# The first window attention: GpSimd stores each block of outputs two steps of its loop later

## The reference, cut to what matters

```python
def _sink_probs(parts, sink):
    snk = jnp.broadcast_to(sink.astype(jnp.float32).reshape(Hk, G)[None, :, :, None, None], base.shape[:-1] + (1,))
    p = jax.nn.softmax(jnp.concatenate(list(parts) + [snk], axis=-1), axis=-1)
    return p[..., :-1]
```

## Time and profile before

| | |
|---|---|
| median of 3 runs | 2663.86 us (2663.03 to 2664.27) |
| profiled execution, its own time | 2663.9 us |
| span of its trace | 2661.8 us (2.1 us of the time lie outside) |
| busy | PE 97%, DVE 57%, ACT 30%, POOL 8% of the span |
| chain of work that ended last | PE 92%, DVE 3%, ACT 2%, issue 2% |
| the window stage | from 167.66 us (first scores) to 353.80 us (first product of the next stage) |

### The profile page before, as it was taken

How to read it: one execution, slowest core, us unless ns; L and a number is a source line. 1 busy time by engine, 2 the same in 40 slices (tenths; PEclk the granted TensorE clock), 3 DMA queues, 4 the chain that set the end, 5 groups by cost and what they waited for, 6 DMA issues and landing times.

```text
span 2661.8 us, 37526 instructions
## 1 busy us (share of the span) xinstructions
PE 2579.5 (97%) x14026; PEld 1886.8 (71%) x14026; DVE 1525.1 (57%) x3904; ACT 802.3 (30%) x1756; POOL 222.7 (8%) x401
## 2 busy tenths in 40 slices
PE   6998899999999999999999999999999999999999
PEld 3476668877768787556678777778678866555867
DVE  2345567579966664434444367657768664514554
ACT  2234521057751123232210046212321275121110
POOL 1100000000000000000024012200000002002000
PEclk9999999999999999999999999999999999999999
DMA  7121000012112222030101010531330103417231
GB/s 261 31 92 45 14 12 33 32 68 75 42 41 72 87 88 79 28 107 9 40 23 44 32 41 24 82 105 56 134 143 33 64 21 90 127 43 258 89 117 55
DMA packets 73058, 188.77 MB, mean 71 GB/s; under 512 B 6988, under 2 KB 9744, under 8 KB 71952
## 3 DMA queue, kind: packets, MB, share of 16 engines
q0 software_dynamic: 26656, 94.84, 11.3%
q1 hardware_dynamic: 45472, 91.16, 9.9%
q10 hardware_dynamic: 752, 0.38, 0.0%
HBM read 143.69 MB, written 43.01 MB: 70 GB/s over the span
## 4 chain that ended last, share of the span: by engine, by line
PE 92%; DVE 3%; ACT 2%; issue 2%; DMA 0%; POOL 0%; ACTq 0%; DVEq 0%
PE psum L1389 35%; PE psum L1721 11%; PE psum L1661 8%; PE psum L1734 7%; PE psum L1752 5%; PE psum L1749 5%; PE psum L1830 4%; PE psum L1603 3%; PE psum L1503 3%; PE psum L1375 2%; PE psum L1356 1%; PE psum L1902 1%; PE psum L1920 1%; PE psum L1889 1%; PE psum L1636 1%
## 5 line engine op out<-in xcount | busy, mean ns | idle before, releaser
L3204 ACT ACTIVATE RP<-RP,small 128x1280 f32<-128x1280 f32 (+11 forms) x274 | 252.4, 923 | 218.6 <-DVE small L2749 182.4
L1721 PE MATMUL psum<-RQ 64*128 64x256 f32 (+5 forms) x1344 | 301.5, 500 | 16.9 <-ACT RP L3217 14.9
L2749 DVE CUSTOM_DVE_ANT_0 RP<-psum,small 128x512 f32<-128x512 f32 (+1 forms) x382 | 202.2, 574 | 123.7 <-PE psum L1734 86.5
L1661 PE MATMUL psum<-RW,hT 128*128 128x512 f32 (+2 forms) x640 | 238.7, 528 | 1.0 <-ACT hT L2954 1.0
L1721 PEld LDWEIGHTS psum<-RQ 64*128 64x128 f32 (+1 forms) x1344 | 147.1, 189 | 106.9 <-issue 57.9
L1734 PE MATMUL psum<-ident,RP 128*128 128x128 f32 x1388 | 195.0, 283 | 8.7 <-DVE RP L2763 3.6
L3217 ACT ACTIVATE RP<-psum 128x512 f32<-128x512 f32 (+1 forms) x304 | 154.6, 525 | 145.9 <-PE psum L1734 135.2
L1661 PEld LDWEIGHTS psum<-RW,hT 128*128 128x128 f32 x640 | 135.6, 216 | 88.1 <-issue 70.4
L1734 PEld LDWEIGHTS psum<-ident,RP 128*128 128x128 f32 x1388 | 153.7, 143 | 62.2 <-issue 53.2
L1389 PE MATMUL psum<-RW,hT 128*128 128x256 f32 x864 | 196.0, 379 | 0.0
L1389 PEld LDWEIGHTS psum<-RW,hT 128*128 128x128 f32 x864 | 163.8, 190 | 25.0 <-issue 2.4
(11 more groups left out here) (485 smaller groups left out, 3945.5 us busy)
## 6 DMA issues: line engine op xcount, KB each, us to landing
RW<-in_w_in SPq DMA_DIRECT2D x7, 2048.0 KB, 8.1
RW<-in_od_w_ada SPq DMA_DIRECT2D x6, 2048.0 KB, 8.0
RW<-in_ev_w_in SPq DMA_DIRECT2D x5, 2048.0 KB, 7.8
RW<-in_od_w_in SPq DMA_DIRECT2D x5, 2048.0 KB, 8.1
RQ<-in_ev_w_ada SPq DMA_DIRECT2D x4, 2048.0 KB, 19.5
RX<-in_x POOLq DMA_DIRECT2D x12, 512.0 KB, 7.7
y_even<-YR POOLq DMA_DIRECT2D x20, 256.0 KB, 2.3
RP<-y_even POOLq DMA_DIRECT2D x20, 256.0 KB, 3.6
```

The lines of the kernel that those rows point to most:

```text
L1661: last = pe.matmul(main.bank(f)[:, 0:nc_], lhs_of(st["lhs"], j["t"], kk), w, start=kk == 0, stop=kk == kn - 1)
L1721: last = pe.matmul(main.bank(f)[:, 0:pc["w"]], q, kk[:, keys], start=i == 0, stop=i == len(u["qk"]) - 1)
L2749: drained(main, dve.tensor_tensor_reduce(pair_slot(st, u, lane)[:, pc["at"]:pc["at"] + pc["w"]], main.bank(f)[:, 0:pc["w"]], add, -scale, ...
L3204: fn(pr, pr, ACT.Exp, bias=mins[:, at, lane, n - 1:n], scale=-1.0, accum_out=sums[:, at, lane:lane + 1]).then_inc(s_pexp, 1)
```

## The change

In the window stage GpSimd's loop runs two steps further than there are pairs. In step `at` it writes the sink columns of pair at+2, as before, and then stores the block of pair at-2, if that is a last pair, instead of that of pair `at`. The wait of the store and its DMA are the same. In the other stages `late` is 0, and the order is as it was.

```diff
-                    for u in ps:
-                        if k == "window" and u["at"] + 2 < len(ps):
-                            sink_columns(ps[u["at"] + 2])
-                        if not u["last"]:
+                    late = 2 if k == "window" else 0
+                    for at in range(len(ps) + late):
+                        if k == "window" and at + 2 < len(ps):
+                            sink_columns(ps[at + 2])
+                        if at < late or not ps[at - late]["last"]:
                             continue
+                        u = ps[at - late]
                         if k == "grid" and u["hp"] + 2 < 4:
                             load_rpb(u["hp"] + 2)
                         b = u["block"]
```

## The result

| | before | after |
|---|---|---|
| median of the runs | 2663.45 us (4 runs, 2661.28 to 2664.27) | 2623.30 us (4 runs, 2620.63 to 2624.70) |
| ratio after / before, 95% interval | | 0.9849 (0.9832 to 0.9866) |
| profiled execution, its span | 2663.9, 2661.8 us | 2623.14, 2621.0 us |
| window stage, first scores to first product of the next stage | 167.66 to 353.80 us, 186.14 us | 167.82 to 314.25 us, 146.43 us |
| behind it, to the end of the span | 2308.0 us | 2306.75 us |

The change saves 40.2 us, 1.5% (36 to 45 us by the interval of the ratio). Predicted were 2623.9 us and a gain of 40.0 us. In the traces the span is 40.8 us shorter: 39.7 us in the stage and 1.25 us behind it. In the code of the changed kernel, lines behind the loop stand two further down: L1734 of before is L1736, L3204 is L3206.

The account below looks back on a forecast made before the run. PE bounds the kernel; in the window stage it stands still nine times because ACT's sinks queue behind GpSimd's store. 2663.9 - 38.4 (gaps and what follows) - 1.6 (stage's end) = 2623.9 us, range 2617 to 2637 us.

Parts of the forecast that it names:

- The sum: Window stage, value products of pair 4 to 37: gapless steps total 119.6 us against 157.97 us recorded, so 38.4 us gained.
- the work aside: Other products PE does within the window stage's steps, one of 16 and two of four: 5.9 us at full clock.
- clean steps: Window-stage steps of PE without a gap, used to build the stage; 3.89 us each for full pairs.
- cut scores: Ahead of the scores, a gap parts the last two of eight products from the other six; 0.85 us, six times.
- The end of the stage: Behind pair 37's values: small gaps stay, but the clock may stay up; 1.6 us gained, by estimate.
- the margin of 3.4 us: ACT wants the first sink behind the store 3.4 us after it comes, 1.4 us among context pairs, so no wait.
- the limit of 16.5 us: Lateness of the store beyond which DVE would wait for its half of YR; 7 us among context pairs.
- rival E: Store leaves too late, DVE waits at blocks 2 to 9 with PE behind: slower, 2680 us if six steps late; chance 0.03.
- GpSimd's writes beside DVE: Moved sinks fall during DVE's minima; the trace was said to differ from the skill's rule; at worst under 4 us.
- B: Window stage: idle time goes but the low clock stays, having another reason than the gaps; 2636.6 us, chance 0.08.
- C: The next or a later stage waits for something not sooner, returning about 20 us; 2644 us, chance 0.06.
- D: A sink behind the store is due at once, so nine waits move by two pairs; 2663.9 us, chance 0.03.

Follow-up runs that it names:

- e2: Against the kernel before: GpSimd waits for the division at the old place but issues the store's DMA two steps later; 2649.47 us.
- e7: Against the kernel before: only the stores of even blocks moved two steps later, the others at the old place; 2637.28 us.
- e3: The kernel before, stores unmoved, with PE's gaps filled by repeating the next pair's first score products; 2645.28 us.
- e1: The changed kernel with the store moved one step later instead of two; 2625.72 us.
- e10: The changed kernel with the store moved one step later instead of two, measured once more in another session; 2623.55 us.
- e5: The changed kernel with the store moved six steps later instead of two; 2624.55 us.
- e6: The changed kernel with the store moved eight steps later instead of two; 2638.33 us.

## Why the prediction was right

- **What bounds it.** The chain from PE's turning back over DVE's division, GpSimd's store and the sinks to ACT, and from ACT's bank to PE, is shown by e2 and e7: moving the store with its wait in a block takes away that block's gap, and moving the DMA's issue alone shortens it by 0.86 us. The links between the engines are the releasers that the rows name.
- **The sum.** 38.4 us for 33 steps were forecast; 157.97 - 119.75 = 38.2 us were measured. That it is so near is luck in the last tenths: the 21 steps of full pairs took 82.0 us and not 81.6, the step from pair 25 to 26 took 3.9 us and not 3.6, and the work aside added 5.3 us and not 5.9 (its two steps took 7.49 and 5.63 us, less two clean ones). The method carried the rest: comparing with clean steps of the same shape counts idle time, low clock and cut scores at once. By the waits of PE alone the forecast would have been 22.3 us, little more than half. e3 shows that the low clock, the larger part of the rest, came from the gaps; the parting of the scores is read from the rows.
- **The end of the stage.** 1.6 us were taken, 6.72 - 5.24 = 1.48 us measured: 8 value products at the end take 0.66 us instead of 1.12 us. What I did not have in the sum is that the low clock also reached into the next stage: its first 32 products take 13.90 us after and took 14.79 us before. That is 0.9 of the 1.25 us behind the stage. The gain has an interval of 36 to 45 us, so that the medians agree with the forecast to 0.2 us is luck too.
- **What is late next.** No wait for the sinks is left, as forecast; the margin of 3.4 us was in truth larger, as e1 and e10 show, and that of 1.4 us among the context pairs was right.
- **The store.** It did not move: after, it is issued behind DVE's division as before. That it could leave a good deal later was right in kind, and e5 and e6 lie on either side of the limit of 16.5 us. The price of rival E, waits of DVE with PE behind them, was seen in e6.
- **GpSimd's writes beside DVE.** Here the prediction misjudged where the rule applies. The Trainium skill's rule ("SBUF — State Buffer", section "Who interferes with whom") is for a VectorE instruction with two inputs from SBUF, and the same section says that one with at most one, outside the modes that take both port pairs, does not contend with GpSimd. The minima read the scores from PSUM and only the mask from SBUF, so 0.61 us with and without sinks beside them agrees with the section and does not differ from it. DVE's busy time from 190 us to the end of the stage is 89.11 us after and 89.75 us before, so it cost nothing that shows.
- **The rivals.** B is refuted by e3; C by the 2306.75 us behind the stage, which are 1.25 us less than before and not 20 us more; D by the waits of ACT; E as it stands in the change by the absence of a wait of DVE for a store.

## What to carry to other kernels

When an engine that runs its stream in order has both a job that others wait for and a job that waits for others, put the second far enough behind the first, within its own deadline, and compute both limits: here one step of lead sufficed, six did no harm, and eight cost 14.8 us. Price a gap of TensorE by the start-to-start distance of the same work with and without it, and not by its idle time, since the slower and parted work behind the gaps cost 16.1 us here on top of 22.3 us of idle time.

## What was not expected of the hardware

- In e2 the granted clock fell to 1.2 GHz directly behind four of nine gaps of 1.55 to 1.75 us; before the change it fell behind six of nine gaps of 2.40 to 2.60 us. In e3 the gaps left were 0.53 to 0.59 us ahead of the scores and 0.67 to 0.87 us ahead of the values, and the clock stayed at 1.00. Why it fell behind some gaps and not behind others of the same length, no run shows.
- The issue of a DMA by GpSimd held up the instructions behind it by 0.86 us a time (36.1 - 28.4 = 7.7 us over nine), while its row shows 0.59 to 0.65 us. About 0.2 us of the difference lies ahead of the row: POOL stands for 12.14 us before its first sink in e2, and in four of the nine for 12.35 or 12.36 us before the store in the kernel before.
